# A transformer layer with expert gathers: 288 of 544 tokens are projected inside the gather loop instead of ahead of it

## What is computed

```python
n = rmsnorm(x, ln1_g)
proj = n @ w_in                       # 8192 columns + 16: qkv, z, lx, ly, ga, gb, bt, dc
qkv, z, lx, ly, ga, gb, bt, dc = split_cols(proj, IN_SPLITS)
qkv_c, dn_buf = causal_conv(qkv, dn_buf0, dn_conv_w)     # 4 taps, then silu
...
o, S = gated_delta_rule(q, k, v, g, beta, S0)            # chunks of 128 tokens, state S
o_a = rmsnorm(o, dn_norm_g) * silu(z)
lc, lru_buf = causal_conv(lx, lru_buf0, lru_conv_w, lru_conv_b)
h, hT = rg_lru(lc, h0, ...)                              # gates by w_r, w_i; a linear scan
o_b = h * gelu(ly)
mix = sigmoid(ga) * (o_a @ w_branch_a) + sigmoid(gb) * (o_b @ w_branch_b)
x = x + mix @ w_out
x = x + peer(rmsnorm(x, ln2_g), peer_w_q, peer_keys, peer_u, peer_v)
```

## Time and profile before

| | us |
|---|---|
| runs, median of 3 (lowest, highest) | 2364.37 (2353.43, 2369.49) |
| the profiled execution | 2363.84 |
| its span, first to last instruction | 2361.7 |
| TensorE busy | 2028.3 |
| VectorE busy | 1432.4 |
| ScalarE busy | 710.1 |
| GpSimd busy | 815.7 |
| bytes moved | 695.82 MB, of which gathers 570.57 MB |

### The profile page before, as it was taken

The page is one execution under the profiler, slowest core; times in us unless marked ns, Lnnn a source line. Parts: engine busy times, 40 slices in busy tenths (PEclk is TensorE's granted clock), DMA queues, the critical chain, the costliest instruction groups (busy, mean ns, idle before and its releaser), DMA issues.

```text
span 2361.7 us, 26994 instructions
## 1 busy us (share of the span) xinstructions
PE 2028.3 (86%) x9678; PEld 1331.2 (56%) x9678; DVE 1432.4 (61%) x3375; ACT 710.1 (30%) x1768; POOL 815.7 (35%) x631
## 2 busy tenths in 40 slices
PE   5999799998867998999988889998999777777776
PEld 5988799997745654555554456654536222322321
DVE  2603802775238974678865658868646667676754
ACT  3454223443114240352341233352312122221221
POOL 3423334440003333334333333334222434444442
PEclk6999899997888999999999999999999999999999
DMA  3212223422368999999999998999889999999997
GB/s 114 90 62 71 91 87 112 146 91 76 111 218 324 349 366 418 413 379 364 390 383 419 406 400 309 356 334 396 345 322 363 385 387 412 401 418 397 381 401 295
DMA packets 129642, 695.82 MB, mean 295 GB/s; under 512 B 14608, under 2 KB 33456, under 8 KB 59136
## 3 DMA queue, kind: packets, MB, share of 16 engines
q0 software_dynamic: 78416, 570.57, 61.6%
q1 hardware_dynamic: 50496, 121.69, 14.6%
q10 hardware_dynamic: 624, 2.23, 0.2%
HBM read 680.31 MB, written 13.61 MB: 294 GB/s over the span
## 4 chain that ended last, share of the span: by engine, by line
PE 45%; DMA 23%; DVE 17%; issue 8%; ACT 3%; POOL 3%; SPq 1%; DVEq 0%; POOLq 0%; ACTq 0%
DMA arena<-in_uv,arena 19%; PE ps L863 18%; PE ps L601 12%; DVE arena L1541 6%; PE ps L784 4%; PE ps L808 2%; DMA arena<-in_w_out 2%; DMA arena<-in_w_a 2%; POOL w_lo L1190 2%; PE ps L735 1%; PE ps L734 1%; PE ps L725 1%; DVE i L1478 1%; ACT arena L1156 1%; DVE v L1475 1%
## 5 line engine op out<-in xcount | busy, mean ns | idle before, releaser
L863 PE MATMUL ps<-arena 128*128 128x512 f32 (+1 forms) x2176 | 1052.8, 622 | 222.2 <-ACT arena L1156 220.6
L1211 POOL DMA_INDIRECT arena<-in_uv,arena x544 | 611.7, 1125 | 1190.9 <-PE ps L863 987.9
L1541 DVE CUSTOM_DVE_ANT_0 arena<-arena 128x1024 f32<-128x1024 f32 x544 | 662.2, 1223 | 426.5 <-DMA arena<-in_uv,arena 420.8
L863 PEld LDWEIGHTS ps<-arena 128*128 128x128 f32 (+1 forms) x2176 | 390.8, 192 | 723.6 <-issue 392.2
L1170 ACT ACTIVATE gelu_d<-dots 128x2 f32<-128x2 f32 x272 | 55.4, 204 | 1057.7 <-DVE dots L1541 1050.5
L601 PE MATMUL ps<-n_hi,w_hi 128*128 128x272 f32 x1024 | 298.5, 292 | 8.2 <-POOL w_lo L1190 8.2
L601 PE MATMUL ps<-n_hi,w_lo 128*128 128x272 f32 x1024 | 299.4, 292 | 0.0
L601 PE MATMUL ps<-n_lo,w_hi 128*128 128x272 f32 x1024 | 297.4, 290 | 0.0
L1190 POOL TENSOR_TENSOR w_lo<-arena,w_hi 128x1024 fp32r<-128x1024 f32 x72 | 188.4, 2617 | 298.4 <-ACT w_hi L919 298.3
L601 PEld LDWEIGHTS ps<-n_hi,w_hi 128*128 128x128 f32 x1024 | 195.9, 191 | 9.0 <-issue 8.1
L601 PEld LDWEIGHTS ps<-n_lo,w_hi 128*128 128x128 f32 x1024 | 196.1, 191 | 0.0
(11 more groups left out here) (232 smaller groups left out, 2127.7 us busy)
## 6 DMA issues: line engine op xcount, KB each, us to landing
arena<-in_stream SPq DMA_DIRECT2D x72, 512.0 KB, 3.3
arena<-in_w_a SPq DMA_DIRECT2D x32, 512.0 KB
arena<-in_w_out SPq DMA_DIRECT2D x32, 512.0 KB
arena<-in_w_q SPq DMA_DIRECT2D x32, 512.0 KB
arena<-in_uv,arena POOLq DMA_INDIRECT x544
spill<-arena SPq DMA_DIRECT2D x12, 512.0 KB, 5.8
arena<-spill SPq DMA_DIRECT2D x4, 1536.0 KB, 11.6
spill<-arena SPq DMA_DIRECT2D x6, 640.0 KB, 7.5
```

What stands on the lines that cost most here:

```text
L863: mm = pe.matmul(ps[0:L, half, :], diag[k % NDIAG][:, 0:L], ring[k % SLOTS][:, D + half * 512:D + (half + 1) * 512], start=False, stop=k % ...
L1211: pool.indirect_dma_start(out=ring[kk % SLOTS], out_offset=None, in_=a["uv"], in_offset=bass.IndirectOffsetOnAxis(ap=idx[:, kk:kk + 1], ax ...
L1541: ins = dve.tensor_tensor_reduce(ring[s][:, 0:D], ring[s][:, 0:D], n2p if t == NTILE else n2[t % 2], 1.0, 0.0, ALU.mult, ALU.add, dots[k / ...
```

## The change

The front now projects tiles 0 and 1 only (N1 = 256 tokens, one product of 256 columns in one bank, banks used by fours). The normalised `n` of the other 288 tokens (tiles 2 and 3 and the samples) goes to DRAM (`spill_n`) and comes back at stage BG. Their projections are 87 new stages (`second_sums`, `second_lru`) in plain fp32, 8 matmuls of 294 columns per chunk, without the split; all 72 chunks and the two gate matrices are transferred a second time, through one list `feed` that also holds the trunk's weights. PACE becomes: slots 1 to 103 tile 1, 104 to 199 the second projections, 200 to 238 tile 2, 239 to 366 tile 3 and samples. LAG goes from 2 to 1 and PICK_AT from (3, 7, 11) to (1, 4, 7). ScalarE and VectorE work on the PSUM banks of the second projections directly: the 3 tokens of history are written into the bank and the convolution reads it from there. Tile 2's results stay in SBUF (`td[2]`), those of tile 3 and the samples go through three staging buffers to DRAM (`spill3`), row by row. Of the old spills only this one is left. Small edits: the parameters are transferred behind x, ln1 and the first four chunks, and the first reciprocal waits for ln1 alone; the convolution of lx adds its bias itself and writes to its place; GpSimd no longer waits for the spills ahead of the first gather.

```diff
-        PICK_AT = (3, 7, 11)
-        LAG = 2
+        PICK_AT = (1, 4, 7)
+        LAG = 1
...
+            if u == 2:
+                BG = stages
+                stages += 87
+                feed += [("stream", CH_LX + n, BG + n) for n in range(KC)]
+                feed += [("gate", j, BG + 17) for j in range(2)]
+                for first, at in ((CH_GA, 18), (CH_Z, 26), (CH_LY, 34)):
+                    feed += [("stream", first + n, BG + at + n) for n in range(KC)]
+                for n in range(KC):
+                    feed += [("stream", CH_GB + n, BG + 44 + 2 * n), ("stream", CH_BB + n, BG + 45 + 2 * n)]
+                feed += [("stream", CH_QKV + m, BG + 60 + m) for m in range(3 * KC)]
...
-        PACE = [(2, 92, BD[1], BD[2]), (92, 220, BD[2], BD[3]), (220, 348, BD[3], stages)]
+        PACE = [(1, 104, BD[1], BG), (104, 200, BG, BD[2]), (200, 239, BD[2], BD[3]), (239, 367, BD[3], stages)]
...
+            sp.wait_ge(n_ready, KC)
+            sp.dma_start(a["spill_n"], n_t[:, :, N1:NT]).then_inc(n_spilled, 16)
...
+                yield BG
+                sp.wait_ge(sc_copied, 2)
+                sp.wait_ge(n_spilled, 16)
+                sp.dma_start(NG[:, :, HIST:HIST + N1], a["spill_n"][:, :, 0:N1]).then_inc(ng_in, 16)
...
                         if s >= unheld:
-                            pe.wait_ge(prod_used, n + (shift - 1))
-                        b = 2 * ((s + shift) % 2)
-                        for half in range(2):
-                            cols = slice(half * HALF, (half + 1) * HALF)
-                            for k in range(KC):
-                                for w, rhs in ((w_hi[s % 2], rhs_hi), (w_hi[s % 2], rhs_lo), (w_lo[s], rhs_hi)):
-                                    mm = pe.matmul(ps[:, b + half, 0:HALF], w[:, k, :], rhs[:, k, cols],
...
+                            pe.wait_ge(prod_used, n + (shift - 3))
+                        for k in range(KC):
+                            for w, rhs in ((w_hi[s % 2], rhs_hi), (w_hi[s % 2], rhs_lo), (w_lo[s], rhs_hi)):
+                                mm = pe.matmul(ps[:, s, 0:N1], w[:, k, :], rhs[:, k, :],
...
+            def second_sums():
+                def product(p, i, rhs, n):
+                    c = group_at(i)
+                    w = wslot[c % RING].rearrange("p (k n) -> p k n", n=P)
+                    pe.wait_ge(chunk_in[c % RING], landed(c))
+                    if p >= 6:
+                        pe.wait_ge(*freed(p - 6))
+                    for k in range(KC):
+                        mm = pe.matmul(ps[:, group_bank(p), 0:n], w[:, k, :], rhs[:, k, :],
+                                       start=(k == 0), stop=(k == KC - 1))
+                    mm.then_inc(tw_used, 1)
+
+                for n in range(KC):
+                    yield BG + n
+                    if n == 0:
+                        pe.wait_ge(sc_copied, 2)
+                        pe.wait_ge(ng_in, uses(2))
+                        pe.wait_ge(ng_zero, 1)
+                    product(n, n, NG, NP2)
...
+                for n in range(3 * KC):
+                    yield BG + 18 + n
+                    product(3 * KC + n, KC + 2 + n, NG, NP2)
...
+                for m in range(3 * KC):
+                    yield BG + 60 + m
+                    product(8 * KC + m, 6 * KC + 2 + m, NG, NP2)
...
-            def evac(j, pr, hist, slot, held):
+            def evac(j, pr, s, held):
...
-                act.copy(x[:, HIST:HIST + HALF], ps[:, b, 0:HALF])
-                act.copy(x[:, HIST + HALF:HIST + TP], ps[:, b + 1, 0:TP - HALF])
-                act.copy(x[:, SMP0:SMP0 + TS], ps[:, b + 1, TP - HALF:HALF]).then_inc(prod_used, 1)
-                act.copy(x[:, TP + HIST:SMP0], hist).then_inc(pad_ready, 1)
...
+                act.copy(xpad[s % 2][:, HIST:HIST + N1], ps[:, s, 0:N1]).then_inc(pad_ready, 1)
+                act.copy(hist1[:, ds(j, 1), :].rearrange("p o n -> p (o n)"), ps[:, s, N1 - HIST:N1]
+                         ).then_inc(prod_used, 1)
...
-            pool.wait_ge(spilled, 18 * 16)
...
-            dve.wait_ge(params_in, N_PARAMS)
+            dve.wait_ge(ln_in, 16)
...
+            def second_sums():
+                def conv(j, p, w):
+                    dve.wait_ge(pad_ready, CONVS + j + 1)
+                    x, y = ps[:, group_bank(p), :], yc[j % 2]
+                    n = NP2 - HIST
...
+                            ins = dve.scalar_tensor_tensor(out=y[:, 0:n], in0=x[:, k:k + n], scalar=w[:, k:k + 1],
+                                                           in1=y[:, 0:n], op0=ALU.mult, op1=ALU.add)
```

More of the change, by code:

```diff
@@ L25 @@
 HIST = CW - 1
[L26 to L29 removed]
+N1 = 2 * P
+N2 = NT - N1
+SMP0 = HIST + N1 + HIST
+NP2 = SMP0 + TS
+YS0 = N1 + HIST
 EPS = 1e-6
@@ L466, in to, with trunk @@
                     self.at += 1
-        def trunk(delta, tail):
-            parts = []
+        def trunk(delta, tail, second):
+            parts = list(second)
             for u in range(NTILE):
@@ L568, in _ @@
+            flow = Weave([loads(), weights(), spills()])
             flow.to(FIRST)
```

621 lines of the change are left out of this document (430 added, 191 removed).

## The result

| | before | after |
|---|---|---|
| median of 4 runs (lowest, highest), us | 2364.84 (2353.43, 2369.49) | 2432.94 (2430.48, 2434.70) |
| profiled execution, us | 2363.84 | 2433.55 |
| its span, us | 2361.7 | 2431.7 |

The changed kernel takes 1.0295 of the time of the one before, 95% interval 1.0257 to 1.0332: 2.9% slower, where 2457 (3.9%) was forecast.

What follows compares the result with a forecast made beforehand. TensorE was taken to bound the front and the DMA engines the gathers, with work moved from first to second. Terms -206 + 25 + 485 - 160 + 0 - 51 = +93 gave 2457 us, 3.9% slower, range 2365 to 2545.

Steps and rivals of the forecast that it cites:

- B: Slots 104 to 199 with the second projections: a new stretch bound by TensorE, +485 us (455 to 530).
- front: Projections and tile 0's trunk before the gathers: GpSimd and ScalarE set the pace, -206 us (-235 to -165).
- E: Last stretch, gathers with hardly any trunk: 177 slots instead of 196 at 2.66 us, -51 us.
- A: Slots 0 to 103 with tile 1's trunk: 12 more slots, less tile 1's read-back, +25 us (15 to 40).
- C: Slots 200 to 238 with tile 2's trunk, dependent steps: 235 us (195 to 300) replacing 395, so -160.
- D: Slots 239 to 366, tile 3 and samples in 128 slots as before: 0 us (-10 to +15).
- rival 3: Clock falls to 1.2 GHz in the new front: 5.05 us a chunk, +90 us, 2547 us; chance 0.05.
- Rival 1: TensorE never waits in front, B and C: 2340 us, 1% faster; chance 0.12 with what lies beyond.
- Rival 2: Tile 2's chain of waits rules C: 300 us plus 15 for first picks, 2537 us; chance 0.12.
- Rival 4: No change: lower ends of front (-235), B (455) and C (210) meet, 2373 us, within 1%; chance 0.11.

Runs made afterwards that it cites:

- k6: The changed kernel with 6 of the 8 matmuls in each woven chunk of the second projections; 2362.54 us (one run).
- k1: The changed kernel with 1 of the 8 matmuls in each woven chunk of the second projections; 2328.29 us (one run).
- conv_psum: The changed kernel with the front's convolution result in two PSUM banks instead of SBUF; 2421.67 us, ratio 1.0283 to the kernel before.
- ng_early: The changed kernel with the spilled n read back during tile 1's tail, into a place of its own; 2431.05 us, ratio 1.0323 to the kernel before.
- f2ng: front2 plus the early read-back of the spilled n during tile 1's tail; 2359.38 us, ratio 0.9972 to the kernel before.
- front2: The changed kernel with the front's convolution result in PSUM and four w_hi buffers instead of two; 2365.05 us, ratio 1.0021 to the kernel before.
- border at 206: f2ng with the border between B and C at slot 206 instead of 200; 2377.18 us against 2359.38.

## Why the prediction was right, and where its terms were off

The sign was right, and so was the mechanism of B, which carries it: k6 and k1 show that TensorE is the bound there and where the gathers' floor lies. The closeness of the whole is partly luck: the 23 us between 2457 and 2434 are what is left of misses in both directions, +23 us in the front, +4 in E, and -10, -26 and -14 in A, C and D. Two of the misses come from one reading: the prediction took a DMA's row in the chain for TensorE's wait, but such a row runs from the issue of the transfer to its landing. TensorE's own waits in the kernel before, for the same three transfers (615 to 665 us, then 900 to 960), are:

```profile
PE ps L784 <- DMA arena<-in_w_a: 5.0, 1, 5.0
PE ps L808 <- DMA arena<-in_w_out: 3.0, 1, 3.0
PE ps L808 <- DMA arena<-in_w_out: 5.2, 1, 5.2
```

- **Front, -206 forecast, -183 measured.** The milestones show where. The scan loop started at 157.75, not 144: lx and ly took 4.3 us a chunk for 3.7, which made ScalarE some 6 us late for the gates (3 of them came back there), and ga was 10 us longer than forecast, with the same table loads, pauses of 2.4 us and slow products (clock 0.86) as z. The loop took 43.5 us for the 45 forecast. branch_b and z took 63.6 us for 60 (pairs of 6.88 in the one, 8.55 in the other), qkv 97 for 91, so the last product came at 362 instead of 340. Where neither a collision nor a table load came in, the prices held: 3.44 a chunk in branch_b against 3.4 forecast. What was mis-sized is the price of a convolved chunk, 3.8: it was taken from the path of two buffers, and the convolution that excludes w_lo sets more. A chunk takes 4.2 in lx and in the later qkv pairs; the mean over qkv is 4.04 (97 / 24), because the first three pairs ran at 3.6 to 3.7 a chunk while VectorE fell behind. By the rule of the Trainium skill, "SBUF — State Buffer", section "Who interferes with whom", the prediction had worked out 3.95 at least, beside the sum. With the steps as measured (2.38 + 3 x 0.49 + 0.35) that working gives 4.2, and this trace agrees with the rule. conv_psum, which takes the second SBUF input away, has 3.59. In the plain groups 3.55 left out the table load in every fourth chunk and what follows it: TensorE, standing longer, comes back at the lower clock for some 3 us. That is rival 3 in part, which had been priced all or nothing (and a little high: 24 products of 0.213 are 5.1 us, not 5.4). Tile 0's trunk alone took 154.6 us (162 before): -8, where -13 was taken for the freed queues. TensorE had waited 5.0 and 3.0 us, not 10.3 and 8.6, and after it does not wait for them at all, which is the 8. (The 29.6 us of waiting ahead of ga is a row of the chain, too; TensorE stood for 1.9 and 5.9 us of them, and no term hangs on it.) And 6 us of pause ahead of the trunk went, which I hadn't seen.
- **A, +25 forecast, +15 measured.** I priced 12 more slots at 2.66 and the missing read-back at 7. A took 3.07 us a slot, against 3.31 before, so the missing read-back was worth more. That it was is argued, not shown, but ng_early puts 1.1 MB back there and pays 8.3 us, and f2ng against front2 12.1.
- **B, +485 forecast, 485.4 measured.** The price that carries it, 4.0 us for a woven chunk, came out at 3.97. That the sum is met to 0.4 us is luck: TensorE was busy 469 for the 460 worked out, the wait for n was 14 for 9, and the 16 us for stages without a chunk and hand-overs were too much by as much. k6 and k1 show both limits.
- **C, 235 forecast, 202.9 measured.** TensorE was busy 182.5 us of 200. I added tile 0's time alone, the add_rows and 25 us for weights, as if nothing of one lay beside the other; the weights cost 7 us of TensorE's waits. The 25 leaned on a wait of 19.2 us for w_out that was 5.2. The chain is real, as the border at 206 shows, but in 39 slots the two still fit nearly on top of each other. The claim that a value under 200 would refute the forecast was close to deciding: two of the changed kernels have 199.7 and 199.9. Six of the 26 us between -160 and -186 are the window's: the stretch before was taken as 395 and is 389.1 by the edges.
- **D, 0 forecast, -14 measured.** All thirteen profiled executions after the change have D between 412 and 421. TensorE's waits in the stretch are 24.4 us before and 14.8 after, its busy time 404 and 400. The chain of before has a transfer of w_a with 15.05 us here, but TensorE waited only 1.7 us for it. No run tried what shortens D, so this stays open.
- **E, -51 forecast, -47 measured.** It scatters from 452 to 464 between executions of these kernels with equal work, which is why 9 us won in B couldn't be told at the end.
- **Rivals.** Rival 1 (TensorE never waits) needed B and C together under 660 us: they took 688. Rival 2 (the chain rules C, 300 us) didn't come about at 202.9; its chain shows only when slots are taken away. Rival 3 came true for a part: clock 0.90 from 41 to 363 us, 0.87 in z. Rival 4 asked for three lower ends; only C's was met.

## What to carry to other kernels

Work moved under another bound is free only up to that bound's own time: in B the gathers alone leave 378 us (k1), and with the fp32 products the stretch took 485. When a stage's main work is halved, look at the helpers that it hid: here one w_lo and one cast per chunk through two buffers, a table load in every fourth chunk and a convolution that w_lo draws out; two more buffers and an output in PSUM gave 66 us back. Take a wait from the engine's own waits, not from a DMA's row in the chain: 10.3, 8.6, 19.2 and 15.05 us there were 5.0, 3.0, 5.2 and 1.7 us of waiting. A pause of TensorE can cost more than its length: ahead of two pairs of z a table load made it 1.2 us longer, and the products behind it lost another 1.5. And in this kernel a stretch of dependent steps was slower both with fewer and with more other slots between them (three borders, in two kernels).
